# Order of the wide and narrow matmuls in the two-row steps of a projection

## The reference, cut to what matters

```python
u = rmsnorm(h, norm_mix_g[l])
proj = u @ w_in[l]
rq, rk, rv, rg, cq, ckv, kr = jnp.split(proj, IN_SPLITS, axis=-1)
...
h = h + jnp.concatenate([ret_out, mla_out], axis=-1) @ w_o[l]
m = rmsnorm(h, norm_mlp_g[l])
h = h + jnp.square(jax.nn.relu(m @ w_up[l])) @ w_down[l]
```

## Time and profile before

| | us |
|---|---|
| median of 3 runs | 1094.96 |
| lowest and highest | 1094.58, 1095.26 |
| the profiled execution | 1094.69 |
| its span, first to last instruction | 1092.8 |

### The profile page before, as it was taken

One profiled execution on the slowest core, in us unless ns is written; L12 is line 12 of the kernel. 1 busy time (PEld: TensorE's weight loads), 2 busy tenths in 40 slices (PEclk: granted clock), 3 DMA queues, 4 the chain that ended last, 5 costly groups with the idle time before them and its releaser, 6 DMA issues.

```text
span 1092.8 us, 15281 instructions
## 1 busy us (share of the span) xinstructions
PE 1078.6 (99%) x6032; PEld 945.1 (86%) x6032; DVE 884.0 (81%) x1243; ACT 671.9 (61%) x1015; POOL 37.9 (3%) x50
## 2 busy tenths in 40 slices
PE   7999999999999999999999999999999999999997
PEld 7899999999988888888888888888888888888886
DVE  7987988888785567789868879887979896889965
ACT  8665766676654556566655566665556655566644
POOL 0001111111100000000000000000000000000000
PEclk9999999999999999999999999999999999999999
DMA  9544444444465545556655555565555665555751
GB/s 339 213 155 154 158 152 157 153 154 155 154 226 198 193 154 195 190 186 204 223 196 193 193 193 186 200 228 193 187 177 182 227 205 198 184 189 187 263 199 77
DMA packets 30311, 206.88 MB, mean 189 GB/s; under 512 B 3488, under 2 KB 3744, under 8 KB 6048
## 3 DMA queue, kind: packets, MB, share of 16 engines
q1 hardware_dynamic: 29952, 205.59, 53.1%
q10 hardware_dynamic: 288, 0.31, 0.1%
HBM read 203.79 MB, written 2.10 MB: 188 GB/s over the span
## 4 chain that ended last, share of the span: by engine, by line
PE 94%; DVE 3%; ACT 1%; DMA 1%; SPq 1%; issue 0%; ACTq 0%
PE acc L433 59%; PE ps_kn L433 8%; PE ps_v L433 7%; PE ps_x L433 5%; PE ps_qn L433 5%; PE ps_qr L433 5%; PE ps_y L433 5%; DMA raw<-w_in 1%; DVE lo L1319 1%; DVE x_sq L1319 0%; SPq L378 0%; ACT x_sq L961 0%; ACT hi L911 0%; SPq L382 0%; DVE rstdx L1428 0%
## 5 line engine op out<-in xcount | busy, mean ns | idle before, releaser
L1319 DVE TENSOR_TENSOR lo<-raw,hi 128x1024 fp32r<-128x1024 f32 (+2 forms) x381 | 459.6, 1214 | 130.0 <-ACT hi L911 125.9
L433 PE MATMUL acc<-xs,hi 128*128 128x512 f32 (+1 forms) x1952 | 539.0, 361 | 0.1
L911 ACT ACTIVATE hi<-raw 128x1024 fp32r<-128x1024 f32 (+2 forms) x381 | 397.9, 1047 | 217.8 <-PE acc L433 100.1
L433 PE MATMUL acc<-xs,lo 128*128 128x256 f32 (+1 forms) x1648 | 357.5, 284 | 7.0 <-DVE xs L1352 7.0
L433 PEld LDWEIGHTS acc<-xs,lo 128*128 128x128 f32 x1648 | 310.6, 188 | 59.8 <-issue 6.9
L433 PEld LDWEIGHTS acc<-xs,hi 128*128 128x128 f32 x1952 | 309.9, 190 | 3.5 <-issue 0.2
L911 ACT ACTIVATE half_b<-acc 128x256 f32<-128x256 f32 x84 | 32.2, 383 | 113.2 <-PE acc L433 113.1
L433 PE MATMUL ps_kn<-hi,act_p 128*128 128x512 f32 x192 | 74.7, 389 | 0.0
L1319 DVE TENSOR_TENSOR t_raw<-raw 128x1024 f32<-128x1024 f32 (+1 forms) x56 | 53.5, 955 | 1.0
L1319 DVE TENSOR_TENSOR z<-acc,half_b 128x256 f32<-128x256 f32 x64 | 27.1, 423 | 31.0 <-ACT half_b L911 31.0
L1319 DVE TENSOR_TENSOR t_lo<-t_raw,t_hi 128x1536 fp32r<-128x1536 f32 x28 | 49.1, 1752 | 0.0
(11 more groups left out here) (383 smaller groups left out, 1512.8 us busy)
## 6 DMA issues: line engine op xcount, KB each, us to landing
raw<-w_up SPq DMA_DIRECT2D x64, 1024.0 KB, 4.8
raw<-w_down SPq DMA_DIRECT2D x64, 1024.0 KB, 4.8
raw<-w_in SPq DMA_DIRECT2D x41, 1024.0 KB, 4.8
raw<-w_o SPq DMA_DIRECT2D x16, 1024.0 KB, 4.8
res<-x_frames SPq DMA_DIRECT2D x1, 2048.0 KB, 8.1
raw<-w_in SPq DMA_DIRECT2D x7, 256.0 KB, 7.8
x_in<-x_all SPq DMA_DIRECT2D x3, 544.0 KB, 7.4
consts<-consts_in SPq DMA_DIRECT2D x1, 1218.5 KB, 9.1
```

The source lines that it names most:

```text
L433: return pe.matmul(o, l, m, start=start, stop=stop)
L911: return act.activation(o, i, ACT.Copy)
L1319: return dve.tensor_tensor(o, a, b, op)
```

## The change

In each step of two row tiles the order of the four matmuls is now the same everywhere: high(n), low(n + 1), low(n), high(n + 1). Before, it was high(n), high(n + 1), low(n), low(n + 1), except in the last step of a block that closes its group, which had high(n), low(n), low(n + 1), high(n + 1). The semaphore still goes with the last matmul of the step.

```diff
                     high(n)
-                    if last and n + 2 == KT:
-                        low(n)
-                        low(n + 1)
-                        m = high(n + 1, True)
-                    else:
-                        high(n + 1)
-                        low(n)
-                        m = low(n + 1)
+                    low(n + 1)
+                    low(n)
+                    m = high(n + 1, last and n + 2 == KT)
                     if n % 8 == 6 and not (late and n == 6):
                         m.then_inc(sem["chunk_used"], 2 if late else 1)
```

## The result

The changed kernel takes 1100.7 us (median of 6 runs, 1099.77 to 1101.6) against 1094.93 for the kernel before in the same comparison: a ratio of 1.0053, 95% interval 1.0043 to 1.0064. It is slower by 5.8 us, outside the forecast range of 1093.0 to 1096.9. The profiled execution took 1101.39 us with a span of 1099.5, 6.7 more than the 1092.8 of before.

A forecast was written before the change was run, and what follows sets the result against it. PE, busy 99% of the span, was taken to bound the kernel. All terms summed to 0, with ends of -2.5 and +3.3 us, so the forecast was 1094.9 us, range 1093.0 to 1096.9.

The forecast's parts named there:

- Item 1, the rotation: Whole block: same four matmuls per pair, each succession of widths 8 times in both orders; 0.692 us a pair, cost 0.
- Item 3, the edge: Step between two blocks, three wide matmuls in a row becoming two: taken as 0, bounds 2.5 us less or more.
- Items 2, 4 and 5: Last pair's narrow matmuls swapped, `chunk_used` moved to a wide matmul, waits unchanged: 0 each; uncovered hand-over 0.8 us.
- The rival of lost cover: Narrow matmuls no longer hide weight loads: 0.013 us for six pairs in 84 blocks, 1101.5 us; chance 0.09 with dearer edge.
- What would make me wrong: A price set by which row tile or weights follow each other, even or odd, not by widths; no size given.

The follow-up runs named there:

- HHLL throughout: Against the kernel before, every pair of every wide block, the last too, runs high(n), high(n+1), low(n), low(n+1): 1093.53 us, ratio 0.9988.

## Why the prediction was wrong

- **What bounds the kernel.** Right: PE sets the end, waits for almost nothing (7.2 us before, 7.7 after, nearly all in the prologue) and has its full clock, before and after. All of the 5.8 us is the pace of PE.
- **Item 1, the rotation.** This is the step that failed: the cost of 0. I counted who follows whom by width and found 8 of each in both orders. The counts were right; but a matmul was taken to have a price by its columns alone. I added that the moving operands come in the same order, n, n+1, n, n+1. True within a pair, but not of the sequence of width and tile in time: before it is wide even, wide odd, narrow even, narrow odd; after, wide odd, wide even of the next pair, narrow odd, narrow even. Even and odd have changed places, and with `xs` at its place they are not alike. In place of 0 the runs showed 0.0133 us per pair, 672 x 0.0133 = 8.9 at most; less what the old tail had cost (1.1 in the profiled spans, 1092.8 against 1091.7 with HHLL throughout) and what pairs behind other work escaped, 6.7 in the profiled spans.
- **Item 3, the edge.** The 0.03 us per block were there and were 0.026. The kernel with HHLL throughout shows that they went with the tail. I had left them at 0 because 512-column matmuls follow each other evenly, and read the place as "three H in a row", a matter of widths. It was the one place in the old trace where the new shape stood, and it had an excess; I didn't ask what eight such pairs would cost. It was a warning and not the price: its narrow matmuls have the other order of tiles, which costs 0.0067 a pair when it runs throughout (89.60), and at other places of `xs` the tail costs nothing.
- **Items 2, 4 and 5.** The hand-over of `chunk_used` and the waits cost nothing that shows: PE has one new wait, of 0.4 us, in the prologue, and none from 61 us on.
- **The rival of lost cover** named 1101.5 us, near the result, from 0.013 us per pair in the rows of the edge. That its price fits is luck, since it came from an edge that isn't the new order's, and its mechanism was wrong: weights in the new order alone give 89.60 and moving operands in the new order 90.45 with the loads in the old one, and moving `xs` by 128 bytes takes the extra away with no load changed.
- **What would make me wrong** named it: a price on which row tile follows which, even or odd. It had no price and no chance, and the range stopped short of it. The moving operand's place beside its order stood nowhere.

The Trainium skill (TensorE: Matmul & The Clock Gate, Back-to-back issue gap) gives an isolated matmul N / 2.4 + 2.5 ns from start to start, an estimate of 0.65 us for the pair, and no term for the operand's place. Here the measured pairs are 0.690 to 0.707, by the place and order of the moving operands; the measurement decides.

**What stays open.** It is shown that the pace of a long stream changes with the place of the moving operands alone, and with their order alone, and that 64 and 192 bytes past a multiple of 256 are not alike. By what rule, isn't: the order H(n) L(n) L(n+1) H(n+1) is the same at three offsets and worse at the fourth, the tail costs nothing at two, even tiles alone took 89.31, 88.35 was reached once, and the block at 281.27 stays at the faster pace. The kernels with one order in each segment, with mixed operands or with other distances ran once each; where a piece of 512 was repeated under the same conditions, within a kernel or between kernels, it agreed within 0.02 us. Why memory does this (which unit reads in what grain) no run shows.

## What to carry to other kernels

When PE runs without a gap, read its pace from start to start, and take an excess at the one place that has the shape of the change as a warning; for the price the sample must have the tiles in the same order too. A sequence of matmuls is not described by its widths: here, with row tiles that start at alternating places within 256 bytes, the order of the tiles was worth up to 1.9% of that stretch (90.45 against 88.75), and a shift of the buffer by 128 bytes turned the slower order into the faster one. So try order and placement together; a change of one that loses may be right at another value of the other.

## What was not expected of the hardware

The pace of a stream of matmuls moved in steps: 0.6933, 0.7000 and 0.7066 us per pair (88.75, 89.60 and 90.45 us for 128 pairs), 0 or 0.0067 or 0.0133 above the best of the kernel's own layout, by the start of the moving operand and its order. With all tiles starting alike, a multiple of 256 bytes was not the best start (89.17 for 512 matmuls; 192 past it 84.61 for 488, the good pace). The order in which the weights were loaded had no part in it: 89.60 and 90.45 with either order of the weights. And the same order at the same place ran at 0.707 a pair in the blocks of the up projection and at 0.693 in one block of the input projection, in three profiles out of three; why isn't shown.
